# Paged attention of the sample group: all keys first, then all values, with keys transposed on VectorE and every page issued from SyncE

## What is computed

```
past_k = cache_k[j, page_table].reshape(nb, -1, DA_HEADS, 2 * DA_DIM)
past_v = cache_v[j, page_table].reshape(nb, -1, DA_HEADS, 2 * DA_DIM)
keys = jnp.concatenate([past_k, k_rows], axis=1).reshape(b, p + s, DA_HEADS, 2, DA_DIM)
vals = jnp.concatenate([past_v, v_rows], axis=1)
s = jnp.einsum('bqhcd,bkhcd->bhcqk', q, k).astype(jnp.float32) * (DA_DIM ** -0.5)
p = jax.nn.softmax(jnp.where(mask, s, -jnp.inf), axis=-1)
w = p[:, :, 0] - lam * p[:, :, 1]
attn = jnp.einsum('bhqk,bkhe->bqhe', w, v)
```

## Time and profile before

| | us |
|---|---|
| median of 3 runs | 2687.76 |
| the runs | 2693.2, 2687.13, 2687.76 |
| the profiled execution, its own time | 2693.54 |
| its span | 2691.9 |
| mean granted TensorE clock, as a share of full speed | 0.992 |

### The profile page before, as it was taken

One profiled execution on the slowest core, in us unless ns is written; L12 is line 12 of the kernel. 1 busy time (PEld: TensorE's weight loads), 2 busy tenths in 40 slices (PEclk: granted clock), 3 DMA queues, 4 the chain that ended last, 5 costly groups with the idle time before them and its releaser, 6 DMA issues.

```text
span 2691.9 us, 49459 instructions
## 1 busy us (share of the span) xinstructions
PE 2623.9 (97%) x20217; PEld 1876.5 (70%) x20217; DVE 1242.1 (46%) x2042; ACT 1026.6 (38%) x1896; POOL 452.3 (17%) x529
## 2 busy tenths in 40 slices
PE   8999899999999999999999999999999999999998
PEld 5666566656688668886566766667657886788765
DVE  5555532326744214444754434344577441154454
ACT  4455322225444214433443333324365441244333
POOL 4001023222022002311101010110101220123121
PEclk9999999999999999999999999999999999999999
DMA  7211369761211312124434242322411122011442
GB/s 250 63 40 50 98 218 346 242 230 54 75 64 32 81 53 63 48 91 146 122 88 88 40 115 50 96 67 84 151 54 67 64 60 60 32 64 48 134 129 97
DMA packets 257659, 266.14 MB, mean 99 GB/s; under 512 B 10668, under 2 KB 217810, under 8 KB 256796
## 3 DMA queue, kind: packets, MB, share of 16 engines
q1 hardware_dynamic: 231772, 166.10, 22.0%
q0 software_dynamic: 25088, 94.79, 10.0%
q10 hardware_dynamic: 576, 2.10, 0.2%
HBM read 227.45 MB, written 35.50 MB: 98 GB/s over the span
## 4 chain that ended last, share of the span: by engine, by line
PE 90%; DVE 5%; ACT 2%; issue 1%; DMA 0%; POOL 0%; SPq 0%; DVEq 0%; ACTq 0%; POOLq 0%
PE ps L372 49%; PE ps L1130 25%; PE ps L1943 2%; PE ps L1931 1%; PE ps L1629 1%; PE ps L1982 1%; PE ps L1708 1%; PE ps L2477 1%; PE ps L2457 1%; PE ps L2491 1%; PE ps L2513 1%; DVE arena L883 1%; PE ps L1694 1%; PE ps L2500 1%; DVE hT L887 1%
## 5 line engine op out<-in xcount | busy, mean ns | idle before, releaser
L372 PE MATMUL ps<-u,w_split 128*128 128x352 f16 (+1 forms) x4752 | 752.3, 315 | 9.8 <-DVE u L737 5.9
L372 PEld LDWEIGHTS ps<-u,w_split 128*128 128x128 f16 (+1 forms) x4752 | 462.5, 98 | 260.3 <-issue 20.8
L372 PE MATMUL ps<-arena,w_split 128*128 128x352 f16 x3663 | 560.6, 313 | 3.7 <-DVE w_split L345 1.5
L372 PEld LDWEIGHTS ps<-arena,w_split 128*128 128x128 f16 x3663 | 357.6, 98 | 200.8 <-issue 9.5
L1130 PE MATMUL ps<-hT,w_split 128*128 128x264 f16 x3456 | 400.6, 276 | 3.2 <-ACT arena L1170 3.2
L1130 PEld LDWEIGHTS ps<-hT,w_split 128*128 128x128 f16 x3456 | 337.8, 98 | 54.8 <-DVE w_split L345 2.1
L345 DVE SCALAR_TENSOR_TENSOR w_split<-w_raw,w_split 128x1024 f16<-128x1024 f32 (+2 forms) x133 | 184.5, 1388 | 296.4 <-ACT w_split L329 295.8
L1130 PE MATMUL ps<-u,w_split 128*128 128x264 f16 x2592 | 303.4, 276 | 0.0
L1130 PEld LDWEIGHTS ps<-u,w_split 128*128 128x128 f16 x2592 | 253.6, 98 | 38.3
L329 ACT ACTIVATE w_split<-w_raw 128x1024 f16<-128x1024 f32 (+2 forms) x133 | 155.5, 1171 | 135.9 <-PE ps L372 97.3
L343 DVE SCALAR_TENSOR_TENSOR w_split<-arena,w_split 128x512 f16<-128x512 f32 x126 | 85.9, 723 | 103.9 <-ACT w_split L323 103.9
(11 more groups left out here) (405 smaller groups left out, 2989.4 us busy)
## 6 DMA issues: line engine op xcount, KB each, us to landing
w_raw<-in_w_down SPq DMA_DIRECT2D x58, 704.0 KB, 4.7
w_raw<-in_w_in SPq DMA_DIRECT2D x56, 512.0 KB, 7.9
arena<-in_w_gu SPq DMA_DIRECT2D x18, 1024.0 KB, 5.3
w_raw<-in_w_gu SPq DMA_DIRECT2D x18, 1024.0 KB, 5.2
hT<-in_cache_k SPq DMA_DIRECT2D x64, 256.0 KB, 4.4
hT<-in_cache_k POOLq DMA_DIRECT2D x64, 256.0 KB, 4.6
hT<-in_cache_v SPq DMA_DIRECT2D x64, 256.0 KB, 5.0
hT<-in_cache_v POOLq DMA_DIRECT2D x64, 256.0 KB, 5.5
```

The costliest lines, as they stand in the source:

```text
L372: ins = pe.matmul(ps[0:m, bank, 0:GW], split_of(v, wp)[:, k * w + col * P:k * w + col * P + m], x[:, xp, k0 + k, cols(g)], start=(k == 0 a ...
```

## The change

- **Order of pages.** First the 128 key pages of all eight sequences, then the 128 value pages. Key loop: 64 steps; value loop: 64 steps. The first softmax lies at key steps 32 to 40, the second at value steps 0 to 8, the first round's output at value steps 32 to 40.
- **Keys.** DVE transposes two pages in one instruction (`dve_turn`: 128 x 1024 float32, in blocks of 32 x 32) from the ring into `turned` (two groups of 4 steps), 4 steps ahead of PE; that frees the two slots. PE has no transposes of keys left, and ACT and DVE no copies of them. Since a block transpose leaves the four blocks of 32 rows of a head's dimension in four partition groups, a group of 8 pages is scored by 64 matmuls of 32 rows x 32 columns with 256 moving columns (4 shifts x 4 heads x 4 partition groups), with the queries in four shifted copies (`q_turned`).
- **Queries.** POOL prepares them earlier, ahead of the last head's stores, and six transfers from SBUF to SBUF make the three shifted copies.
- **Queues.** Every page is issued from SP: 16 in a row early, then 240 in a row. The weight tiles that were woven between them (loads 19 to 27) are issued from ACT's queue, in `act_proj0`. POOL issues no page.
- **Buffers.** `probs`, the turned weights and `comb` lie elsewhere; each round has its own weights and its own output bank (6 and 3).
- **Weaving.** `SAMPLE_FILL` spreads the same 54 halves: 28 over the tail and the key steps, 26 after them.

```diff
+        O_BANK = (6, 3)
+        turned = [rows(19 + 4 * i, 4)[:, :, 0:SEQ] for i in range(2)]
...
+                if v >= CXB + 3 and g == 1:
+                    load_tile(act, v + 4)
...
+        def dve_turn(dve, q):
+            f = 2 * q
+            dve.wait_ge(page_loaded[f % RING // 2], 32 * (f // RING + 1))
+            if q >= 8:
+                dve.wait_ge(scored, q // 4 - 1)
+            dve.transpose(turned[q // 4 % 2][:, q % 4, :],
+                          ring[:, f % RING:f % RING + 2, :].rearrange("p r c -> p (r c)")).then_inc(page_used, 2)
...
+            pool.wait_ge(q_copied, 2 * NB)
+            for s_ in range(1, 4):
+                cut = P - 32 * s_
+                pool.dma_start(arena[0:cut, Q_ROWS[s_], 0:SEQ], arena[32 * s_:P, Q_ROWS[0], 0:SEQ]).then_inc(q_ready, 16)
+                pool.dma_start(arena[cut:P, Q_ROWS[s_], 0:SEQ], arena[0:32 * s_, Q_ROWS[0], 0:SEQ]).then_inc(q_ready, 16)
+
+        SAMPLE_FILL = ((1, 1, 0)
+                       + ((0, 0, 0, 1) + (0, 0, 0, 2)) * 3 + (0, 0, 0, 1) + (0, 0, 0, 4)
+                       + ((0, 0, 0, 1) + (0, 0, 0, 2)) * 4
+                       + (0, 0, 2, 0, 0, 0) * 10 + (0, 0, 2, 1)
+                       + (1, 1, 1))
 
         def load_page(eng, f):
 
-            cache, b, p = (cache_k, cache_v)[f // 64 % 2], 4 * (f // 128) + f // NPG % 4, f % NPG
+            cache, b, p = (cache_k, cache_v)[f // (NB * NPG)], f // NPG % NB, f % NPG
...
         def sp_samples(sp):
...
+            for f in range(RING, 2 * NB * NPG):
+                load_page(sp, f)
...
+            def scores(n):
+
+                b, j = n // 2, n % 2
+                pe.wait_ge(page_used, 8 * n + 8)
+                pe.wait_ge(exps, 9 * (n // 8))
+                pages = turned[j].rearrange("p a (e c) -> p a e c", e=2)
+                for s_ in range(4):
                     for h in range(HEADS):
+                        for i in range(4):
+                            part_, e0 = slice(32 * i, 32 * i + 32), P * h + 32 * ((i + s_) % 4)
+                            ins = pe.matmul(ps[32 * h:32 * h + 32, i, 256 * j:256 * j + 256],
+                                            q_turned[s_][part_, h, b, :], pages[part_, :, :, e0:e0 + 32],
+                                            start=(b % 4 == 0 and j == 0 and s_ == 0),
+                                            stop=(b % 4 == 3 and s_ == 3), skip_group_check=True)
+                ins.then_inc(scored, 1)
...
+            for q in range(64):
+                if q % 4 == 3:
+                    scores(q // 4)
+                if q % 32 == 31:
+                    own_scores(q // 32)
+                if q == 35:
+                    first_weights(0)
+                if q == 39:
+                    last_weights(0)
+                yield
...
             for f in range(RING):
-                if f // 2 % 2 == 0:
-                    load_page(sp, f)
+                load_page(sp, f)
             for v in range(5, CXB + 7):
                 load_tile(sp, v)
-            woven(sp_samples(sp), sp_proj0(sp, CXB + 3, WO0 - 1), SAMPLE_FILL)
+            sp_samples(sp)
```

More of the change, by code:

```diff
@@ L1849, in dve_head @@
                     yield
+                if h == HEADS - 1 and i == 7:
+                    dve_turn(dve, 0)
                 if i < 7:
@@ L1998, in pe_samples @@
                 ins.then_inc(os_t, 1)
-                yield
+            for q in range(64):
[7 more added lines that the diff above has]
+                    last_weights(0)
+                yield
+            for q in range(64):
+                values(q)
+                if q == 3:
+                    first_weights(1)
+                if q == 7:
+                    last_weights(1)
+                if q == 39:
+                    out_turned(0)
+                yield
+            yield
+            yield
+            out_turned(1)
+            yield
         def act_samples(act):
@@ new lines, in exponentials @@
+            def exponentials(r_):
+                act.wait_ge(max_ready, r_ + 1)
+                for i in range(4):
+                    for a in range(2):
+                        act.activation(probs[a].rearrange("p (f i t) -> p i f t", i=4, t=32)[:, i],
+                                       ps[:, i, 256 * a:256 * a + 256].rearrange("p (f t) -> p f t", t=32), ACT.Exp,
+                                       bias=sm_neg, accum_out=sm_sum[:, 2 * i + a:2 * i + a + 1]).then_inc(exps, 1)
+                act.activation(probs_own, ps[:, 4, 0:TS], ACT.Exp, bias=sm_neg,
+                               accum_out=sm_sum[:, 8:9]).then_inc(exps, 1)
@@ L2112, in dve_samples @@
                 ins.then_inc(os_lo, 1)
-                yield
+            for q in range(128):
+                if q in (32, 64):
+                    maxima(q // 32 - 1)
+                if q in (33, 65):
+                    scales(q // 32 - 1)
+                if 5 <= q + 4 < 64:
+                    dve_turn(dve, q + 4)
+                if q in (36, 68):
+                    own_copied(q // 32 - 1)
+                if q in (40, 72):
+                    weights_copied(q // 32 - 1)
+                if q == 97:
+                    out_sums(0)
+                if q == 99:
+                    out_scaled(0)
+                if q == 104:
+                    out_low(0)
+                yield
+            out_sums(1)
+            out_scaled(1)
+            yield
+            yield
+            out_low(1)
+            yield
         hn = mix
@@ L2858, in _ @@
             pool.dma_start(v_s[0].rearrange("b t h e -> (b t) h e"), kv_s_nat[1]).then_inc(rows_saved, 16)
-            for f in range(RING, 2 * NB * NPG):
-                if f // 2 % 2:
-                    load_page(pool, f)
             pool.wait_ge(page_used, 2 * NB * NPG)
```

259 lines of the change are left out of this document (101 added, 158 removed).

## The result

| | before | after |
|---|---|---|
| median of the runs | 2687.85 us (4 runs, 2687.13 to 2693.2) | 2719.86 us (4 runs, 2714.79 to 2722.5) |
| the profiled execution | 2693.54 us, span 2691.9 | 2720.69 us, span 2718.9 |
| mean granted TensorE clock | 0.992 | 0.977 |

The changed kernel is slower: ratio 1.0113, 95% interval 1.0099 to 1.0126. In medians that is +32 us, and from profile to profile +27.1, against the forecast of +15. The forecast had the sign and the place right; the size is about twice what was said.

What follows compares the result with a forecast made beforehand. The bound was to move from PE to SP's issue of pages at 1.10 us each; 13.9 us for the stage plus 1 for early pages gave 15, so 2708.5 profiled and a median of 2703 us, range 2694 to 2730.

Steps and rivals of the forecast that it cites:

- upper end of 2.46: DVE's key transposes: at most two full passes, 2.46 us per instruction; 1.23 was taken.
- upper end 9.1: PE's key scores: 9.1 us per group of 64 matmuls if row groups don't overlap at all; 2.3 was taken.
- The sum: Sample stage: 231 page intervals of 1.10 us on SP, landing and last values delay the last matmuls by 13.9 us.
- At nothing: the softmaxes: Key step 32: DVE's transposes wait some 10 us behind the softmax; the ring covers 12, so no cost.
- the cover of 12 us: 16-page ring at the softmaxes: 17.6 us of SP's time, 12 left after landing and transposes; more delays SP.
- SP waits for a slot after 320 us: SP's queue in the sample stage: any such wait would show the prediction wrong; it expected SP never held after page 24.
- half of the last values' work: End of the value steps: 0.6 us between the last page's landing and the start of the last matmuls.
- the same 11 us: From the last values' matmuls to the output projection: 11 us as before, with 3 halves kept back in both.
- The early pages: 16 instead of 8 pages on SP ahead of visit 5's weights: up to 4 us later, 1 taken.
- A, SP keeps up: Sample stage: issues overlap, PE bounds, 47 us less, 2641; faster below 1.04 us a page; chance 0.05.
- B: Sample stage: earlier page 24, quicker landing and slack behind leave at most 7 us, 2691 to 2695, no change; chance 0.10.
- C: Sample stage: slow transposes or score matmuls add 29 to 49 us, softmax holds or lower clock some us each; chance 0.12.

Runs made afterwards that it cites:

- experiment 1: The changed kernel with page pairs alternating between SP's and POOL's queues again: 2675.97 us, ratio to the kernel before 0.9954.
- experiment 2: The changed kernel with the page's number loaded twice for every page after the first 16: 2834.74 us, one run.
- experiment 4: The changed kernel without the bounds check of the page's number, still on one queue: 2675.76 us, ratio to the kernel before 0.995.
- experiment 7: The changed kernel with two queues and seven halves moved from key steps to value steps: 2667.95 us, ratio to the kernel before 0.992.
- experiment 3: The kernel before with every page issued from SP and nothing else of the change: 2737.3 us, ratio to the kernel before 1.0182.

## Why the prediction was right in kind and wrong in size

The median was forecast at 2703 us and came out at 2719.86: 17 us are missing, of which 12.1 lie in the sum for the profile and 5 in the step from the profile to the median.

**What held.** The bound moves from PE to SP's issue, the price is 1.10 us a page, and PE's saving turns into waits for pages: SP's median distance between issues in the changed kernel is 1.10 us, and experiments 1, 2 and 4 move the time with it in both directions. The bounded prices came out near the values taken. A transpose takes 1.24 us, forecast 1.23, and the upper end of 2.46 was far off. A group of 64 score matmuls takes 2.69 us, forecast 2.3, upper end 9.1: row groups do overlap. The timeline of PE, where the group at full clock starts at 410.31 and its successor at 413.00 (a matmul of float32 counts as two):

```profile
410.31 2.76 PE L1931 MATMUL ps<-arena 32*32 32x256 f32 x128
413.00 1.96 PE L372 MATMUL ps<-u,w_split 128*128 128x352 f16 x12
```

On the transpose, the row shows 1244 ns for 1024 float32 in each partition, 1.21 ns each: as long as the two-operand pass of the earlier trace rows, and longer than the one-operand pass of 0.75 us. The Trainium skill says in "Vector Engine (DVE) Microarchitecture Reference", section 3.8, that a transpose sustains one element per cycle per lane. The trace agrees in that one pass is all that the transpose takes, where the upper end had two; how long the engine's cycle is, no row shows.

**What failed: the step "The sum", its term 231 x 1.10 = 254.1 us.** The rate between neighbours was right, and it is not the mean. From page 24, issued at 315.52 (3.2 us earlier than forecast, 2.8 of it because the evacuation ahead of the first transpose starts at 301.17 instead of 303.95), to page 255 at 581.95 are 266.4 us, 1.153 each and 12.3 more than 254.1. The timeline of SP at page 24, at the first softmax and at two pairs in the value steps:

```profile
315.52 1.78 SPq L1900 DMA_DIRECT2D hT<-in_cache_k  x2
...
385.42 4.77 SPq L1900 DMA_DIRECT2D hT<-in_cache_k  x4
...
537.61 1.79 SPq L1900 DMA_DIRECT2D hT<-in_cache_v  x2
...
541.26 1.44 SPq L1900 DMA_DIRECT2D hT<-in_cache_v  x2
```

A pair is 1.10 + 0.34 = 1.44 us, as at 541.26. Some pairs are 1.78: SP's queue stops for some 0.3 us between two instructions. This happens eleven times, each 21 or 22 pages apart, and costs 3.3 us in all. Sixteen DMA instructions last clearly longer than their 0.338 us, up to 1.23, for 4.7 us in all (line 1900 of the changed kernel, duration ns min/median/max):

```profile
L1900 SPq DMA_DIRECT2D hT<-in_cache_k x128: 332/338/1231, 44.0 to 436.6; - x128
```

The step "At nothing: the softmaxes" failed with it: halves, partly at the lower clock, stand ahead of the first softmax's maxima and take the cover of 12 us away, and page 88 and page 90 are held, 3.5 us. SP waits for a slot after 320 us, which the forecast had named as a sign that it is wrong. The first shows in the row at 385.42, 4.77 us for four pages that would take 3.64. The three make 11.5 of the 12.3. The row that the forecast took its 1.10 from spanned two intervals; the row of eight beside it had 1.16, and was put aside as holding one longer instruction. Over 231 pages such instructions are part of the price: 1.16 would have given 268, within 2 us of the 266.4 measured. That nearness is in part luck: without the 3.5 us of holds the mean is 1.138.

The first softmax shows why the cover was thinner (timeline of PE, 378 to 398 us):

```profile
379.78 5.62 PE L372 MATMUL ps<-u,w_split 128*128 128x352 f16 x24 [5.31 <-DVE arena L1599]
392.65 4.71 PE L1931 MATMUL ps<-arena 32*32 32x256 f32 x128 [7.25 <-ACT small L2028]
```

Two halves take 5.62 us, at a granted clock of 0.66 from 379.8 to 385.4 us and behind 5.31 us of idle time, where such a pair takes 3.75 at full clock; the evacuation that waits for them stands on VectorE ahead of the maxima, and these ahead of the transposes that free the slots.

**What failed besides: the 0.6 us of "half of the last values' work", and "the same 11 us" behind the stage.** Between the last issue and the closing matmul lie 8.4 us instead of 4.6, since two halves, 5.97 us at 0.61 of the clock, stand ahead of the last value step: +3.8. At full clock they would be 2.2 us shorter (3.75), so 2.2 of the 3.8 are the clock, and the rest is where they stand. The stretch from there to the output projection is 12.8 instead of 10.8 us: +1.9. "Since 3 halves are kept back for it in both" was misread: the changed kernel has four there, at 590.68 (two in a row), 595.78 and 598.00, since the last value step is followed by one half in its table, and before by none. The half at 595.78 besides waits for an evacuation that now stands behind the norming of the sums on VectorE. Which of the two counts isn't separated: experiment 7 has three halves there and still takes 12.5 us (540.84 to 553.31), with PE idle 2.84 us for that evacuation. Of the 1.9, 1.7 come back when the projection's first 72 matmuls take 10.91 us, at full clock, instead of 12.59 us at 0.86 of it. The early pages were put at 1 us and cost nothing: ACT's split of the late weights starts at 67.40, 1.1 us later than before, and PE is not behind there. At 301 us the trace even stands 2.8 us ahead of that of before. This comes with the rest of the change and not with the queue: the same evacuation starts at 301.2 to 302.7 us in all eight kernels that have the rest, and at 304.97 in experiment 3, which has the queue alone. Which part of the rest does it, no run separates.

Together, against the 15 us: -3.2 + 12.3 + 3.8 + 1.9 - 1.7 - 1 = 12.1, and 15 + 12.1 = 27.1, the distance of the two profiles. The other 5 us of the medians' 32 come from a step that looked harmless: the profiled execution before stood 5.8 us above its median, and the forecast took the same off for the changed kernel, whose profiled execution stood 0.8 above.

**The rivals.** *A, SP keeps up*, was right in that a page well below its 1.04 us makes the kernel faster (experiment 4, at 0.81 unheld). Its size was not: it gave -47 us, and with the queue out of the way the change is worth -14 (experiment 1), -21 with a fill made for it (experiment 7). The forecast had counted PE's work alone; in experiment 1 PE is idle for 23 us of the key steps, behind the softmax, VectorE and waits with no releaser, and waits 14.7 us for pages in the value steps. What each of these costs at the end isn't shown. *B* is excluded by the interval. *C* fell in its large parts: neither the transposes nor the row groups are slow. Its small ones came true, as a part of the missing 12.1 us: 3.5 of holds at the first softmax, and some 2.2 of the 3.8 at the end, by the clock. The 8.0 of stops (3.3) and long instructions (4.7) are the queue's own, and these no rival had.

**The rule that was weighed.** In the changed kernel one issue costs 1.10 us (median) and a transfer 262,144 bytes at the best rate seen, 0.72. The Trainium skill ("DMA: Bandwidth & Descriptors", section "Issuing engines are not separate DMA queues") says that several issuers save only the sequencer's time, usually small relative to the DMA itself. Its first half agrees with the runs: what a second queue saves is the sequencer's time. Its "usually small" does not hold here: that time is 44 us of the kernel (experiment 1), and as much when it is cut on one queue (experiment 4).

## What to carry to other kernels

Multiply the cost of one issue by the number of transfers of the stage before moving them to one queue: at 1.10 us for a page whose number is read from the table, a queue moves 238 GB/s of 256 KB pages at best, however idle it looks, and here dropping an instruction pair from the issue (with the check that it makes) was worth as much as a second queue, 44 us. Take the mean over a long unheld stretch, stops and long instructions included, and not the distance between neighbours, when it is multiplied by hundreds. A saving on the engine that bounds a stage is worth only the distance to the next bound; when PE fell idle between pieces here, its work also got dearer, 5.97 us instead of 3.75 for two halves, so the places of filler work must be set anew.

## What the runs showed of the hardware that was not expected

SP's queue stops for some 0.3 us at a fixed count of its instructions. At 6 instructions a page (the trace shows a MOVE of 0.03 us beside the five that the program's list has) the stops come each 21 or 22 pages (11 in 231 pages), at 9 instructions a page (experiment 2) each 14 or 15 pages (16 in the same stretch), at 4 instructions (experiment 4) each 32 pages (7): in all three exactly once per 128 instructions of the queue. What the queue does in the stop, no row shows.

A stage whose pages come too slowly shows a granted clock down to 0.73 in its windows, where before it showed 0.99, and so filler work that had been free gets onto the path: the 24 matmuls of two halves take 3.75 us at full clock, and 5.62 or 5.97 where PE had idled ahead of them and was granted 0.66 and 0.61.
